# Leaving rows of zero weight out of the gathers of a routed expert layer, made head by head, with five added rows in eight on TensorE

## The chip, the cores and the metric

The kernel runs on one core of one Trainium2 chip. The metric is the time of the core on the device in microseconds (us), from the first to the last instruction. Three runs of the kernel before were made, and their median is what the changed kernel is compared with.

## The reference, cut to what matters

A model of several blocks on 256 tokens of width 2048 in float32: an attention block, a Fourier mixer, a convolution and state-space mixer, a cross attention, and at the end a layer of routed experts. Only the last is touched. In it each of 8 heads picks 16 of 128 x 128 experts for each token, so a token has 128 experts; each expert is one row of 2048 numbers in a table `u_tab` (here called scored rows) and one in a table `v_tab` (added rows):

```python
g = jax.nn.softmax(top_s, axis=-1)                 # of the 16 best scores of a head
u = jnp.take(u_tab, it, axis=0)                    # scored rows, one per token and slot
act = jax.nn.gelu(jnp.einsum("td,tkd->tk", xt, u))
v = jnp.take(v_tab, it, axis=0)                    # added rows
return jnp.einsum("tk,tkd->td", gt * act, v)       # weight = gt * act
```

The inputs are random, and several are multiplied by a factor: the gain of the layer's norm by 8, the scored table by 3.246, the query weights by 2.935, the keys by 2.911. A weight `gt * act` is exactly zero in float32 where gelu of a negative product is, or where the softmax term vanishes. The result goes through a last norm.

## The kernel before

Everything ahead of the expert stage is untouched and ends some 2100 us into the run. The stage (class `Experts`, functions `g_experts`, `v_experts`, `a_experts`, `pe_experts`) treats the 256 tokens as two tiles (t = 0, 1) of 128 tokens, one token per SBUF partition. For each tile there are 128 slots k (`E_SLOTS`), 16 (`TOPK`) for each of 8 heads. A gather is one indirect DMA that GpSimd (POOL) issues (L3784): for one (t, k) it brings one row of 8 KB for each of 128 tokens, from `in_peer_u` (table 0, scored) or `in_peer_v` (table 1, added). There are 512. They go into twelve buffers of 8 KB per partition (four in `arena`, eight in `ring`), used in a fixed rotation; a gather waits until what its buffer held was used.

`ORDER`, written by `gather_order`, is the one order in which all engines go through the gathers: first `LAG` = 36 scored ones, then one added and one scored in turn, and at the end added ones alone (36).

- VectorE (DVE) sums a scored row against the token's input with one instruction (`v_scored`, L3698), which gives one product per token in `X.act`.
- When the 32 scored rows of two heads are done, ScalarE (ACT) applies gelu to their 32 products (L3741), and DVE, just before the first added row of those two heads, multiplies them by the softmax terms (L3681). These are the weights.
- An added row is taken by DVE, as weight x row + sum in place (L3686), or by TensorE (PE): ACT builds a diagonal matrix of the weights (L3750, four buffers `diag`), and PE multiplies it by the row into four PSUM banks (L3554, four calls, each of which is two instructions in the trace). Of eight slots, `PE_ROWS` = 1, 4 and 6 go to PE.
- Between them DVE makes the choice of experts for the next two heads in small steps (`v_choose`, L3566 to L3646), whose integer row numbers `X.idx` the gathers read.
- When the last added row of a tile is done, `v_finish` adds PE's sums to DVE's, takes the norm and scales (L3709 to L3715), and the tile is stored.

In the kernel before, an added gather waits only for the row numbers and for its buffer, not for the weights.

Of the kernel before, what the change touches and what calls it, by code (L numbers as in the profile page):

```python
# [39 lines left out]
HH = 2  # L40
# [3344 lines left out]
class Experts:  # L3385
    def __init__(self, c):
        W = c.I["peer_w_q_2"][0]
        n = HH * 2 * E_HALF
        self.q_lins = [Lin(f"peer_q{g}", W, g * n, (g + 1) * n) for g in range(GROUPS)]
        self.H = c.at(0, NT, D)  # L3390
        self.hn = c.at(4 * K1, NT, D)
        self.x = c.at(8 * K1, KD * SEQ)
        self.f_row = c.at(10 * K1, D)
        self.g_row = c.at(12 * K1, D)
        self.rs = c.st[:, 62:64]
        self.qT = c.at(12 * K1, E_HEADS, SEQ)
        self.keys = c.at(14 * K1, E_HEADS, E_KEYS)
        self.sc = c.at(15 * K1, HH * 2, E_KEYS)
        self.cand = c.at(15 * K1 + 512, HH, TOPK, TOPK)
        self.eq = c.at(16 * K1, HH, TOPK, TOPK)  # L3400
        small = c.at(21 * K1, 16, 256)
        self.v1 = small[:, 0, :]
        self.i1 = small[:, 1, :].bitcast(U32)
        self.i1f = small[:, 2, :]
        self.top = small[:, 3, 0:E_SLOTS]
        self.pos = small[:, 4, 0:E_SLOTS].bitcast(U32)
        self.pi = small[:, 5, 0:E_SLOTS].bitcast(U32)
        self.pj = small[:, 6, 0:E_SLOTS].bitcast(U32)
        self.pif, self.pjf = small[:, 7, 0:E_SLOTS], small[:, 8, 0:E_SLOTS]
        self.e1, self.e2 = small[:, 9, 0:E_SLOTS], small[:, 10, 0:E_SLOTS]  # L3410
        self.idxf = small[:, 11, 0:E_SLOTS]
        self.hsum = small[:, 12, 0:E_HEADS]
        self.g = c.at(25 * K1, NT, E_SLOTS)
        self.act = c.at(25 * K1 + 256, NT, E_SLOTS)
        self.idx = c.at(25 * K1 + 512, NT, E_SLOTS).bitcast(U32)
        self.bufs = [c.ring[:, i // 2, (i % 2) * D:(i % 2 + 1) * D] for i in range(2 * RING)] + [
            c.at(17 * K1, D), c.at(19 * K1, D), c.at(26 * K1, D), c.at(28 * K1, D)]
        self.buf_of = {}
        self.tables = (c.I["peer_u_2"][0], c.I["peer_v_2"][0])
        self.sums, self.added, self.diag_holder = {}, None, {}  # L3420

    def diag_of(self, t, k):

        return sum(1 for j in range(k) if on_pe(j)) % 4

    def cols(self, k):
        return self.x[:, k * SEQ:(k + 1) * SEQ]
# [3 lines left out]
        return [key for q in (ch // 4, ch // 4 + 1) for key in turn_free(("ffn_x", q), 4, NT)]  # L3431


LAG = HH * TOPK + 4
PE_ROWS = (1, 4, 6)


def gather_order():
# [10 lines left out]
ORDER = gather_order()  # L3449


def on_pe(k):

    return k % 8 in PE_ROWS


LAST_PE_ROW = max(k for k in range(E_SLOTS) if on_pe(k))


def choice_at(t, k):  # L3460
# [69 lines left out]
def pe_experts(c):  # L3530
    nc, pe, X = c.nc, c.pe, c.experts
    last_rows = pe_ffn_rows(c)(KD // 4 - 1)
    for h in range(HH):
        yield from pe_queries(c, X, h, 1, None if h else last_rows)
        yield from pe_choose(c, X, 0, h, 1)
    for h in range(HH, E_HEADS, HH):
        yield from pe_queries(c, X, h, HH)
        if h == HH:
            yield from pe_choose(c, X, 0, h)
    for n, (t, table, k) in enumerate(ORDER):  # L3540
        if table == 0:
            choice = choice_at(t, k)
            if choice is not None and choice[2] == 0 and choice[:2] != (0, 1):
                yield from pe_choose(c, X, choice[0], choice[1] * HH)
            continue
        if k == PE_ROWS[0]:
            X.sums[t] = []
            for b in range(4):
                bank = yield from pe_bank(c, c.lin, ("rows", t, b))
                X.sums[t].append(bank)  # L3550
        if on_pe(k):
            yield from pe.wait_ge(("diag", t, k), ("got", t, 1, k))
            for b in range(4):
                mm = nc.tensor.matmul(X.sums[t][b][:, :], c.diag[:, X.diag_of(t, k), :],  # L3554
                                      X.buf_of[t, 1, k][:, b * 512:(b + 1) * 512],
                                      start=(k == PE_ROWS[0]), stop=(k == LAST_PE_ROW), skip_group_check=True)
            names = [("full", ("rows", t))] if k == LAST_PE_ROW else []
            mm.then_inc(c.pe_full.after(("row_used", t, 1, k), *names), 1)


# [95 lines left out]
def v_experts(c):  # L3656
    nc, v, X, step = c.nc, c.v, c.experts, c.v_step
    vt = nc.vector.tensor_tensor
    yield from v_ffn_rows(c, KD // 4 - 1)
    yield from v_ffn_gained(c, KD // 4 - 1)  # L3660
    yield from v_rms(c, "ffn_x", ("y_mem", "squares"))
    nc.vector.tensor_copy(X.rs, c.st[:, 0:NT]).then_inc(step.after(("ffn_x", "scale")), 1)
    for h in range(HH):
        if h == 0:
            yield from v_copy_out(c, ("query", h), X.qT[:, h, :], lambda: c.bank[("query", h)][:, 0:SEQ])
        v.side = [v_choose(c, X, 0, h, 1)]
        yield from v.aside(0)
    for n, (t, table, k) in enumerate(ORDER):
        if table == 0:
            yield from v_scored(c, X, t, k)  # L3670
            choice = choice_at(t, k)
            if choice is not None:
                if choice[2] == 0:
                    v.side = [v_choose(c, X, choice[0], choice[1] * HH)]
                yield from v.aside(1)
            continue
        group = k // (HH * TOPK)
        if k % (HH * TOPK) == 0:
            ks = slice(k, k + HH * TOPK)
            yield from v.wait_ge(("gelu", t, group))  # L3680
            nc.vector.tensor_tensor(X.act[:, t, ks], X.act[:, t, ks], X.g[:, t, ks], ALU.mult).then_inc(  # L3681
                step.after(("weights", t, group)), 1)
            yield from v.wait_ge(step)
        if not on_pe(k):
            yield from v.wait_ge(("got", t, 1, k), X.added)
            nc.vector.scalar_tensor_tensor(out=X.H[:, t, :], in0=X.buf_of[t, 1, k], scalar=X.act[:, t, k:k + 1],  # L3686
                                           in1=X.H[:, t, :], op0=ALU.mult, op1=ALU.add).then_inc(
                c.v_out.after(("row_used", t, 1, k)), 1)
            X.added = ("row_used", t, 1, k)
        if k == E_SLOTS - 1:  # L3690
            yield from v_finish(c, X, t)


def v_scored(c, X, t, k):
    yield from c.v.wait_ge(("got", t, 0, k))
    buf = X.buf_of[t, 0, k]
    names = [("scored", t, k // (HH * TOPK))] if k % (HH * TOPK) == HH * TOPK - 1 else []
    c.nc.vector.tensor_tensor_reduce(out=buf, in0=buf, in1=X.hn[:, t, :], scale=1.0, scalar=0.0, op0=ALU.mult,  # L3698
                                     op1=ALU.add, accum_out=X.act[:, t, k:k + 1]).then_inc(
        c.v_out.after(("row_used", t, 0, k), *names), 1)  # L3700
# [18 lines left out]
def a_experts(c):  # L3719
# [10 lines left out]
    for h in range(HH, E_HEADS, HH):  # L3730
        yield from a_copy_out(c, ("query", h), X.qT[:, h:h + HH, :], lambda: pairs(c.bank[("query", h)][:, :]))
    for n, (t, table, k) in enumerate(ORDER):
        group = k // (HH * TOPK)
        if table == 0:
            choice = choice_at(t, k)
            if choice is not None and choice[2] == 9:
                yield from a_choose(c, X, choice[0], choice[1] * HH)
            if k % (HH * TOPK) == HH * TOPK - 1:
                ks = slice(k + 1 - HH * TOPK, k + 1)
                yield from a.wait_ge(("scored", t, group))  # L3740
                nc.scalar.activation(X.act[:, t, ks], X.act[:, t, ks], ACT.Gelu_apprx_tanh, scale=X.rs[:, t:t + 1]).then_inc(  # L3741
                    c.a_step.after(("gelu", t, group)), 1)
                if (t, group) == (NT - 1, GROUPS - 1):
                    yield from a_root_ahead(c)
            continue
        if on_pe(k):
            q = X.diag_of(t, k)
            yield from a.wait_ge(("weights", t, group), X.diag_holder.get(q))
            X.diag_holder[q] = ("row_used", t, 1, k)
            nc.scalar.activation(c.diag[:, q, :], c.ident[:, :], ACT.Copy, scale=X.act[:, t, k:k + 1]).then_inc(  # L3750
                c.a_step.after(("diag", t, k)), 1)
# [12 lines left out]
def g_experts(c):  # L3764
# [13 lines left out]
    for n, (t, table, k) in enumerate(ORDER):  # L3778
        m = n - FIRST_ROUNDS * len(early)
        q = early[n % len(early)] if m < 0 else order[m % len(order)]  # L3780
        yield from g.wait_ge(("idx", t, k // TOPK), holder.get(q))
        holder[q] = ("row_used", t, table, k)
        X.buf_of[t, table, k] = X.bufs[q]
        c.nc.gpsimd.indirect_dma_start(  # L3784
            X.bufs[q], None, X.tables[table],
            bass.IndirectOffsetOnAxis(ap=X.idx[:, t, k:k + 1], axis=0)).then_inc(got[q].after(("got", t, table, k)), 16)


def program(nc, I, out):
# [151 lines left out]
```

## Time and profile before

| | |
|---|---|
| runs | 3407.87, 3407.84, 3405.35 us, median 3407.84 |
| span of the profiled execution | 3407.9 us; the time of its run lies within 0.1 us of it |
| DMA in the expert stage | 421 to 422 GB/s |
| DVE busy in the whole span | 2503.4 us |
| POOL busy in the whole span | 1497.5 us |
| PE busy in the whole span | 2574.2 us |

The profile is of one execution. Times are in us from the start of the span, durations of single instructions in ns where marked. In the slices a digit is the busy share in tenths (9 is 90% or more), each slice being a fortieth of the span, 85.2 us. PEclk is the clock granted to TensorE, DMA the mean busy share of the core's 16 DMA engines. The duration of a DMA instruction on POOL is the time in which POOL makes its descriptors, not the transfer; the time to landing is the transfer with its queue.

### The profile page before, as it was taken

How to read it: one execution, taken by the hardware profiler on the slowest of the kernel's cores; microseconds unless marked ns; L12 is line 12 of the kernel's file. 1: busy time of each engine (PE TensorE's matmuls, PEld its weight loads, DVE VectorE, ACT ScalarE, POOL GpSimd, SP SyncE). 2: the span in 40 equal slices, each digit the busy share in tenths (PEclk: the TensorE clock that was granted, in tenths of full speed). 3: DMA queues.
4: the chain of work that ended last, by engine and by line, in shares of the span. 5: the costliest groups of instructions: out<-in, count | busy, mean ns of one | idle time of the engine just before them, and what ended most of it. 6: DMA issues, size and time to landing. Idle time of an engine off the chain costs nothing.

```text
span 3407.9 us, 32819 instructions
## 1 busy us (share of the span) xinstructions
PE 2574.2 (76%) x11844; PEld 1856.5 (54%) x11844; DVE 2503.4 (73%) x3758; ACT 1004.3 (29%) x1999; POOL 1497.5 (44%) x1973
## 2 busy tenths in 40 slices
PE   6999999999999999999999999144444444444445
PEld 4678886557888887887677888111111111111112
DVE  5568887756677765568756557997878888888775
ACT  5364263233555444444155442000000001000000
POOL 6678888700000000002200002887777767777663
PEclk9999999999999999999999999576766766676778
DMA  9967766525477755554635556999999999999998
GB/s 377 387 233 288 251 216 230 222 105 181 151 246 248 233 189 179 173 200 164 188 132 174 172 174 241 412 422 422 421 421 422 422 421 414 420 421 422 421 422 333
DMA packets 297858, 986.05 MB, mean 289 GB/s; under 512 B 15456, under 2 KB 139744, under 8 KB 213216
## 3 DMA queue, kind: packets, MB, share of 16 engines
q0 software_dynamic: 77024, 555.78, 39.4%
q1 hardware_dynamic: 216448, 417.56, 35.7%
q10 hardware_dynamic: 4224, 10.62, 0.8%
q8 instruction: 93, 1.52, 0.2%
q14 instruction: 69, 0.57, 0.1%
HBM read 965.94 MB, written 17.96 MB: 289 GB/s over the span
## 4 chain that ended last, share of the span: by engine, by line
PE 52%; DMA 17%; DVE 14%; POOL 10%; issue 4%; ACT 3%; SPq 0%; ACTq 0%; DVEq 0%
PE lin L568 12%; DMA ring<-in_peer_v,arena 7%; POOL ring L3784 7%; PE lin L493 6%; PE lin L495 6%; PE lin L494 6%; PE lin L570 6%; DMA ring<-in_peer_u,arena 4%; PE lin L394 3%; POOL arena L3784 3%; PE lin L3554 3%; DMA arena<-in_peer_u,arena 3%; DMA arena<-in_peer_v,arena 3%; DVE scratch L915 2%; DVE weight_parts L451 2%
## 5 line engine op out<-in xcount | busy, mean ns | idle before, releaser
L451 DVE TENSOR_TENSOR weight_parts<-ring,weight_parts 128x512 fp32r<-128x512 f32 (+2 forms) x994 | 671.5, 689 | 468.5 <-ACT weight_parts L439 463.8
L439 ACT CAST weight_parts<-ring 128x512 fp32r<-128x512 f32 (+2 forms) x994 | 593.4, 607 | 699.1 <-PE lin L495 357.9
L3554 PE MATMUL lin<-ring,scratch 128*128 128x512 f32 x512 | 362.0, 873 | 493.9 <-DMA ring<-in_peer_v,arena 372.5
L568 PE MATMUL lin<-parts,weight_parts 128*128 128x512 f32 x1792 | 643.3, 402 | 12.6 <-DVE weight_parts L451 9.8
L3554 PEld LDWEIGHTS lin<-ring,scratch 128*128 128x128 f32 x512 | 140.1, 287 | 712.6 <-issue 656.5
L570 PE MATMUL lin<-parts,weight_parts 128*128 128x256 f32 x1792 | 503.4, 281 | 0.0
L3698 DVE CUSTOM_DVE_ANT_0 ring<-ring,arena 128x2048 f32<-128x2048 f32 x168 | 383.3, 2289 | 92.3 <-DMA ring<-in_peer_u,arena 86.4
L493 PE MATMUL lin<-weight_parts,parts 128*128 128x512 f32 (+2 forms) x1092 | 419.1, 384 | 24.4 <-DVE weight_parts L451 16.8
L3784 POOL DMA_INDIRECT ring<-in_peer_u,arena x168 | 301.5, 1795 | 306.3 <-DVE arena L3571 231.3
L494 PE MATMUL lin<-weight_parts,parts 128*128 128x512 f32 (+2 forms) x1092 | 410.3, 376 | 0.0
L495 PE MATMUL lin<-weight_parts,parts 128*128 128x512 f32 (+2 forms) x1092 | 410.1, 376 | 0.0
L568 PEld LDWEIGHTS lin<-parts,weight_parts 128*128 128x128 f32 x1792 | 338.8, 189 | 111.2 <-DVE weight_parts L451 16.6
L3784 POOL DMA_INDIRECT ring<-in_peer_v,arena x172 | 303.7, 1766 | 160.4 <-PE lin L3554 112.4
L3554 PE MATMUL lin<-arena,scratch 128*128 128x512 f32 x256 | 178.9, 864 | 217.0 <-DMA arena<-in_peer_v,arena 186.8
L570 PEld LDWEIGHTS lin<-parts,weight_parts 128*128 128x128 f32 x1792 | 340.6, 190 | 0.4
L3686 DVE SCALAR_TENSOR_TENSOR arena<-ring,arena 128x2048 f32<-128x2048 f32 x108 | 253.6, 2348 | 33.9 <-DMA ring<-in_peer_v,arena 32.5
L493 PEld LDWEIGHTS lin<-weight_parts,parts 128*128 128x128 f32 x1092 | 207.9, 190 | 76.4 <-DVE weight_parts L451 23.1
L3554 PEld LDWEIGHTS lin<-arena,scratch 128*128 128x128 f32 x256 | 69.6, 286 | 325.3 <-issue 288.7
L1094 POOL DMA_DIRECT2D arena<-mem_turned x3 | 1.6, 541 | 539.2 <-PE aux L2323 529.0
L3698 DVE CUSTOM_DVE_ANT_0 arena<-arena 128x2048 f32<-128x2048 f32 x88 | 200.9, 2288 | 50.8 <-DMA arena<-in_peer_u,arena 47.9
L495 PEld LDWEIGHTS lin<-weight_parts,parts 128*128 128x128 f32 x1092 | 207.9, 190 | 36.7
L494 PEld LDWEIGHTS lin<-weight_parts,parts 128*128 128x128 f32 x1092 | 207.8, 190 | 35.5 <-issue 1.2
(329 smaller groups left out, 3846.1 us busy)
## 6 DMA issues: line engine op xcount, KB each, us to landing
ring<-in_ada_row_loads SPq DMA_DIRECT2D x64, 1024.0 KB, 8.3
ring<-in_w_in_fourier SPq DMA_DIRECT2D x64, 1024.0 KB, 8.4
ring<-in_ada_front_loads SPq DMA_DIRECT2D x32, 1024.0 KB, 8.6
ring<-in_w_in_attn SPq DMA_DIRECT2D x32, 1024.0 KB, 7.0
ring<-in_w_out_fourier SPq DMA_DIRECT2D x16, 2048.0 KB, 8.0
ring<-in_w_in SPq DMA_DIRECT2D x24, 1024.0 KB, 7.4
ring<-in_mem_k_loads SPq DMA_DIRECT2D x16, 1024.0 KB, 10.9
ring<-in_w_out_attn SPq DMA_DIRECT2D x8, 2048.0 KB, 7.9
```

The lines of the kernel that those rows point to most:

```text
L394: mm = c.nc.tensor.matmul(banks[j // 2][:, (j % 2) * SEQ:(j % 2 + 1) * SEQ], wt[:, k % L.kc, j * P:(j + 1) * P], rhs(k), start=(k == 0 and ...
L439: c.nc.scalar.copy(c.w_parts[:, q, 0, 0:L.per * w], weights_of(c, L, load, w, k)).then_inc(c.a_high.after(("high", L.name, i)), 1)
L451: c.nc.vector.tensor_tensor(c.w_parts[:, q, 1, 0:L.per * w], weights_of(c, L, load, w, k), c.w_parts[:, q, 0, 0:L.per * w].bitcast(F32), A ...
L493: c.nc.tensor.matmul(banks[t][:, 0:w], lhs(0, k, t), hi, start=(k % part == 0), stop=False)
L494: c.nc.tensor.matmul(banks[t][:, 0:w], lhs(0, k, t), lo, start=False, stop=False)
L495: mm = c.nc.tensor.matmul(banks[t][:, 0:w], lhs(1, k, t), hi, start=False, stop=(k % part == part - 1))
L568: c.nc.tensor.matmul(pairs(banks[j][:, :]), c.w_parts[:, q, 0, b], x, start=(k == 0), stop=False, skip_group_check=True)
L570: mm = c.nc.tensor.matmul(banks[j][:, hi_at * SEQ:(hi_at + 1) * SEQ], c.w_parts[:, q, 1, b], x[:, hi_at, :], start=False, stop=(k == L.K - ...
L3554: mm = nc.tensor.matmul(X.sums[t][b][:, :], c.diag[:, X.diag_of(t, k), :], X.buf_of[t, 1, k][:, b * 512:(b + 1) * 512], start=(k == PE_ROW ...
L3686: nc.vector.scalar_tensor_tensor(out=X.H[:, t, :], in0=X.buf_of[t, 1, k], scalar=X.act[:, t, k:k + 1], in1=X.H[:, t, :], op0=ALU.mult, op1 ...
L3698: c.nc.vector.tensor_tensor_reduce(out=buf, in0=buf, in1=X.hn[:, t, :], scale=1.0, scalar=0.0, op0=ALU.mult, op1=ALU.add, accum_out=X.act[ ...
L3784: c.nc.gpsimd.indirect_dma_start(X.bufs[q], None, X.tables[table], bass.IndirectOffsetOnAxis(ap=X.idx[:, t, k:k + 1], axis=0)).then_inc(go ...
```

## The change

1. Weights are made for each head (16 slots) and not for two heads, and sooner: `weights_at` places them four places behind the head's last scored row in `ORDER` (`WEIGHTS_BEHIND` = 4), in a new function `v_weights`. ACT's gelu is applied for each head as well.
2. `v_weights` then compares the weights with zero, gives zero ones a row number out of the table (`NO_ROW`, 4 x 128 x 128) and writes the row numbers of the head anew, as integers.
3. Added gathers wait for these row numbers (`rows_needed`) and carry a bounds check: a row number above 16383 brings no row, and the buffer keeps what it held there. Its weight is zero.
4. Five of eight added rows are PE's (slots 1, 2, 4, 6, 7) in place of three; in the last 32 added rows, behind which no scored ones stand, it is three as before.
5. 32 scored gathers stand ahead of the first added one, not 36, and so 32 added ones are alone at the end.

```diff
-LAG = HH * TOPK + 4
-PE_ROWS = (1, 4, 6)
+LAG = 2 * TOPK
+PE_ROWS = (1, 2, 4, 6, 7)
+PE_ROWS_ALONE = (1, 4, 6)
+WEIGHTS_BEHIND = 4
+NO_ROW = 4 * E_KEYS * E_KEYS
...
+def on_pe(t, k):
+
+    alone = (t, k) >= (NT - 1, E_SLOTS - LAG)
+    return k % 8 in (PE_ROWS_ALONE if alone else PE_ROWS)
...
+def weights_at(n):
+
+    last = [(t, 0, k) for t in range(NT) for k in range(TOPK - 1, E_SLOTS, TOPK)]
+    done = ORDER[n - WEIGHTS_BEHIND] if n >= WEIGHTS_BEHIND else None
+    return (done[0], done[2] // TOPK) if done in last else None
...
     for n, (t, table, k) in enumerate(ORDER):
+        due = weights_at(n)
+        if due is not None:
+            yield from v_weights(c, X, *due)
...
-        group = k // (HH * TOPK)
-        if k % (HH * TOPK) == 0:
-            ks = slice(k, k + HH * TOPK)
-            yield from v.wait_ge(("gelu", t, group))
-            nc.vector.tensor_tensor(X.act[:, t, ks], X.act[:, t, ks], X.g[:, t, ks], ALU.mult).then_inc(
-                step.after(("weights", t, group)), 1)
-            yield from v.wait_ge(step)
-        if not on_pe(k):
+        if not on_pe(t, k):
...
+def v_weights(c, X, t, h):
+
+    nc, v, step = c.nc, c.v, c.v_step
+    ks = slice(h * TOPK, (h + 1) * TOPK)
+    yield from v.wait_ge(("gelu", t, h))
+    nc.vector.tensor_tensor(X.act[:, t, ks], X.act[:, t, ks], X.g[:, t, ks], ALU.mult).then_inc(
+        step.after(("weights", t, h)), 1)
+    yield from v.wait_ge(step)
+    nc.vector.tensor_scalar(X.skip, X.act[:, t, ks], 0.0, float(NO_ROW), ALU.is_equal, ALU.mult).then_inc(step.after(), 1)
+    yield from v.wait_ge(step)
+    nc.vector.tensor_tensor(X.idxf[:, ks], X.idxf[:, ks], X.skip, ALU.max).then_inc(step.after(), 1)
+    yield from v.wait_ge(step)
+    nc.vector.tensor_copy(X.idx[:, t, ks], X.idxf[:, ks]).then_inc(step.after(("rows_needed", t, h)), 1)
...
-        c.nc.gpsimd.indirect_dma_start(
-            X.bufs[q], None, X.tables[table],
-            bass.IndirectOffsetOnAxis(ap=X.idx[:, t, k:k + 1], axis=0)).then_inc(got[q].after(("got", t, table, k)), 16)
+        if table == 0:
+            yield from g.wait_ge(("idx", t, k // TOPK), holder.get(q))
+            c.nc.gpsimd.indirect_dma_start(X.bufs[q], None, X.tables[0], rows).then_inc(
+                got[q].after(("got", t, 0, k)), 16)
+        else:
+            yield from g.wait_ge(("rows_needed", t, k // TOPK), holder.get(q))
+            c.nc.gpsimd.indirect_dma_start(X.bufs[q], None, X.tables[1], rows, bounds_check=E_KEYS * E_KEYS - 1,
+                                           oob_is_err=False).then_inc(got[q].after(("got", t, 1, k)), 16)
```

## Rows read from the trace of the kernel before

**Rows 1.** Page, 40 slices of the span: POOL, DMA share and rate.

```profile
POOL 6678888700000000002200002887777767777663
DMA  9967766525477755554635556999999999999998
GB/s 377 387 233 288 251 216 230 222 105 181 151 246 248 233 189 179 173 200 164 188 132 174 172 174 241 412 422 422 421 421 422 422 421 414 420 421 422 421 422 333
```

**Rows 2.** Busy time of each engine in the four stretches of the stage.

```profile
core 0: us, PE busy (x) PEld busy (x) DVE busy (x) ACT busy (x) POOL busy (x), PEclk, DMA share, GB/s
2102.00:2185.00 83.00, 38.28 (x187) 32.94 (x185) 80.89 (x157) 3.67 (x6) 62.46 (x36) 0.75 0.98 398
2185.00:3279.00 1094.00, 471.71 (x683) 183.97 (x684) 921.24 (x1024) 50.64 (x117) 808.89 (x440) 0.68 1.01 421
3279.00:3370.00 91.00, 53.47 (x93) 21.38 (x92) 58.69 (x33) 6.59 (x16) 52.98 (x37) 0.79 1.01 421
3370.00:3408.00 38.00, 18.95 (x35) 7.03 (x33) 22.42 (x20) 3.49 (x10) 0.58 (x1) 0.80 0.54 222
```

**Rows 3.** Page, DMA queue of POOL: packets, MB, share of 16 engines.

```profile
q0 software_dynamic: 77024, 555.78, 39.4%
```

**Rows 4.** Line 3784 (gathers): duration ns min/median/max, first and last start; landing.

```profile
L3784 POOL DMA_INDIRECT ring<-in_peer_v,arena x172: 932/1894/5215, 2185.4 to 3369.6; - x172
L3784 POOL DMA_INDIRECT ring<-in_peer_u,arena x168: 933/1906/5215, 2102.1 to 3279.2; - x168
DMA to landing us min/median/max: 6.6/23.6/26.7
```

**Rows 5.** Windows of 2400 to 3200: all engines, then lines 3698 and 3686.

```profile
2400.00:3200.00 800.00, 353.07 (x508) 137.79 (x509) 670.77 (x753) 38.30 (x89) 582.22 (x321) 0.68 1.01 421
...
2400.00:3200.00 800.00, 364.21 (x319) 0.68 1.01 421
...
2400.00:3200.00 800.00, 232.92 (x100) 0.68 1.01 421
```

**Rows 6.** Timeline, DVE and POOL, 2130 to 2136: start us, us.

```profile
2130.68 2.28 DVE L3698 CUSTOM_DVE_ANT_0 ring<-ring,arena 128x2048 f32<-128x2048 f32 x1
2130.82 2.95 POOL L3784 DMA_INDIRECT ring<-in_peer_u,arena  x1 [0.30 <-issue]
2132.89 2.28 DVE L3698 CUSTOM_DVE_ANT_0 arena<-arena 128x2048 f32<-128x2048 f32 x1
2134.08 1.91 POOL L3784 DMA_INDIRECT ring<-in_peer_u,arena  x1 [0.30 <-issue]
2135.10 0.86 DVE L3581 MAX8 arena<-arena 128x8 f32<-128x128 f32 x4
```

**Rows 7.** Timeline, DVE and POOL, 2503 to 2506.

```profile
2503.71 0.94 POOL L3784 DMA_INDIRECT arena<-in_peer_v,arena  x1 [0.30 <-issue]
2504.95 0.94 POOL L3784 DMA_INDIRECT arena<-in_peer_u,arena  x1 [0.30 <-issue]
2505.27 2.29 DVE L3698 CUSTOM_DVE_ANT_0 ring<-ring,arena 128x2048 f32<-128x2048 f32 x1 [2.68 <-DMA ring<-in_peer_u,arena]
```

**Rows 8.** Timeline of PE, an added row's instructions after a pause and later.

```profile
2512.86 3.38 PE L3554 MATMUL lin<-ring,scratch 128*128 128x512 f32 x4 [2.44 <-DMA ring<-in_peer_v,arena]
...
3372.49 3.67 PE L3554 MATMUL lin<-arena,scratch 128*128 128x512 f32 x8 [1.30 <-DMA arena<-in_peer_v,arena]
```

**Rows 9.** Lines 3681 (weights) and 3750 (diagonals): duration ns min/median/max.

```profile
L3681 DVE TENSOR_TENSOR arena<-arena x8: 183/186/191, 2210.0 to 3316.6; 128x32 f32<-128x32 f32 x8
...
L3750 ACT ACTIVATE scratch<-ident,arena x96: 384/386/403, 2210.2 to 3371.2; 128x128 f32<-128x128 f32 x96
```

**Rows 10.** Chain that ended last, its end: start us, us.

```profile
3369.64 24.98 DMA ring<-in_peer_v,arena
...
3394.65 2.36 DVE arena L3686
...
3397.10 0.70 DVE arena L3709
```

More of the change, by code:

```diff
@@ L3412, in __init__ @@
         self.hsum = small[:, 12, 0:E_HEADS]
+        self.skip = small[:, 13, 0:TOPK]
         self.g = c.at(25 * K1, NT, E_SLOTS)
@@ L3422, in diag_of @@
     def diag_of(self, t, k):
-        return sum(1 for j in range(k) if on_pe(j)) % 4
+        return sum(1 for j in range(k) if on_pe(t, j)) % 4
     def cols(self, k):
@@ L3449 @@
 ORDER = gather_order()
-def on_pe(k):
-    return k % 8 in PE_ROWS
-LAST_PE_ROW = max(k for k in range(E_SLOTS) if on_pe(k))
+def on_pe(t, k):
+    alone = (t, k) >= (NT - 1, E_SLOTS - LAG)
+    return k % 8 in (PE_ROWS_ALONE if alone else PE_ROWS)
+LAST_PE_ROW = [max(k for k in range(E_SLOTS) if on_pe(t, k)) for t in range(NT)]
+def weights_at(n):
+    last = [(t, 0, k) for t in range(NT) for k in range(TOPK - 1, E_SLOTS, TOPK)]
+    done = ORDER[n - WEIGHTS_BEHIND] if n >= WEIGHTS_BEHIND else None
+    return (done[0], done[2] // TOPK) if done in last else None
 def choice_at(t, k):
@@ L3550, in pe_experts @@
                 X.sums[t].append(bank)
-        if on_pe(k):
+        if on_pe(t, k):
             yield from pe.wait_ge(("diag", t, k), ("got", t, 1, k))
@@ L3555, in pe_experts @@
                                       X.buf_of[t, 1, k][:, b * 512:(b + 1) * 512],
-                                      start=(k == PE_ROWS[0]), stop=(k == LAST_PE_ROW), skip_group_check=True)
-            names = [("full", ("rows", t))] if k == LAST_PE_ROW else []
+                                      start=(k == PE_ROWS[0]), stop=(k == LAST_PE_ROW[t]), skip_group_check=True)
+            names = [("full", ("rows", t))] if k == LAST_PE_ROW[t] else []
             mm.then_inc(c.pe_full.after(("row_used", t, 1, k), *names), 1)
@@ L3696, in v_scored @@
     buf = X.buf_of[t, 0, k]
-    names = [("scored", t, k // (HH * TOPK))] if k % (HH * TOPK) == HH * TOPK - 1 else []
+    names = [("scored", t, k // TOPK)] if k % TOPK == TOPK - 1 else []
     c.nc.vector.tensor_tensor_reduce(out=buf, in0=buf, in1=X.hn[:, t, :], scale=1.0, scalar=0.0, op0=ALU.mult,
@@ L3732, in a_experts @@
     for n, (t, table, k) in enumerate(ORDER):
-        group = k // (HH * TOPK)
+        h = k // TOPK
         if table == 0:
@@ L3737, in a_experts @@
                 yield from a_choose(c, X, choice[0], choice[1] * HH)
-            if k % (HH * TOPK) == HH * TOPK - 1:
-                ks = slice(k + 1 - HH * TOPK, k + 1)
-                yield from a.wait_ge(("scored", t, group))
+            if k % TOPK == TOPK - 1:
+                ks = slice(k + 1 - TOPK, k + 1)
+                yield from a.wait_ge(("scored", t, h))
                 nc.scalar.activation(X.act[:, t, ks], X.act[:, t, ks], ACT.Gelu_apprx_tanh, scale=X.rs[:, t:t + 1]).then_inc(
-                    c.a_step.after(("gelu", t, group)), 1)
-                if (t, group) == (NT - 1, GROUPS - 1):
+                    c.a_step.after(("gelu", t, h)), 1)
+                if (t, h) == (NT - 1, E_HEADS - 1):
                     yield from a_root_ahead(c)
             continue
-        if on_pe(k):
+        if on_pe(t, k):
             q = X.diag_of(t, k)
-            yield from a.wait_ge(("weights", t, group), X.diag_holder.get(q))
+            yield from a.wait_ge(("weights", t, h), X.diag_holder.get(q))
             X.diag_holder[q] = ("row_used", t, 1, k)
@@ L3780, in g_experts @@
         q = early[n % len(early)] if m < 0 else order[m % len(order)]
-        yield from g.wait_ge(("idx", t, k // TOPK), holder.get(q))
+        rows = bass.IndirectOffsetOnAxis(ap=X.idx[:, t, k:k + 1], axis=0)
+        X.buf_of[t, table, k] = X.bufs[q]
+        if table == 0:
[6 more added lines that the diff above has]
+                                           oob_is_err=False).then_inc(got[q].after(("got", t, 1, k)), 16)
         holder[q] = ("row_used", t, table, k)
-        X.buf_of[t, table, k] = X.bufs[q]
-        c.nc.gpsimd.indirect_dma_start(
-            X.bufs[q], None, X.tables[table],
-            bass.IndirectOffsetOnAxis(ap=X.idx[:, t, k:k + 1], axis=0)).then_inc(got[q].after(("got", t, table, k)), 16)
 def program(nc, I, out):
```

## The prediction

> **What bounds the kernel now.** I read the 40 slices first, to find where the changed code runs. In the slices from the 26th on, the DMA engines are nine tenths or more busy and move about 422 GB/s; that is the expert stage, the only one whose code differs [rows 1]. Then the windows cut at the stage's own joints: 2102 to 2185 (scored rows alone), 2185 to 3279 (an added row and a scored row in turn), 3279 to 3370 (the last added rows) and the end. In the second the DMA engines are full (share 1.01), DVE is busy for 921 of 1094 us, POOL for 809 and PE for 472 [rows 2]. The reader is to see that the transfers set the pace and that three other engines stand at 43 to 84%. 220 added and 220 scored gathers go in 1094 us, so a pair takes 4.97 us, and one gather of 128 rows of 8 KB (1.0486 MB) takes 2.49 us at 421 GB/s. The queue of POOL's transfers confirms it: 555.8 MB, of which the 512 gathers are 536.9 [rows 3]. A gather lands a median 23.6 us after its issue, some nine gathers of 2.49 us deep [rows 4]. So POOL runs ahead of the transfers, and a saving of bytes is a saving of time until another engine is as slow.
>
> **The bytes that go.** An added row is left out when its weight is exactly zero. The trace can't show how many are, so I took the reference's arithmetic with its inputs. The normalised input has a gain of about 8 and the scored table a factor of 3.246, so the products have a spread of 8 x 3.246 = 26, and gelu is zero in float32 below about -5.2: two fifths of a spread of 26 lies there (the normal share below -0.2 is 42%). Evaluated on the inputs, 44.0% of the 32,768 weights are zero, 2 points of it from softmax terms that vanish. That is 14,400 rows. In single gathers it is 30 to 58%. It assumes that the engine's gelu and exp reach exact zero at about those places. An added gather then takes 0.56 x 2.49 = 1.39 us, and a pair 2.49 + 1.39 = 3.88 us of the DMA engines. Over 256 added gathers 256 x 0.44 x 2.49 = 280 us of transfer go. If nothing else bound, the time would be 3408 - 280 = 3128 us.
>
> **DVE.** In 2400 to 3200 it is busy 670.8 us for 161 pairs, 4.17 us each; 364.2 are the scored rows' sums (2.29 each) and 232.9 the added rows (2.35 each) [rows 5]. Three added rows in eight stay on DVE in place of five: 0.25 x 2.35 = 0.59 us less in a pair. The new weights take four small instructions for a head of 16 rows where one of 0.19 us stood for 32 [rows 9]; at 0.19 each with their waits some 0.8 us a head, 0.05 a pair. So 4.17 - 0.59 + 0.05 = 3.63 us: below 3.88, no bound by itself.
>
> **PE.** An added row is eight instructions. Four that follow a pause take 3.38 us, 0.85 each, and all eight of a row on a busier engine 3.67 us, 0.46 each [rows 8]; the granted clock is 0.68 on average in the stage [rows 2], between the two levels of 1.2 and 2.4 GHz. Five rows in eight are 0.625 x 3.67 = 2.3 us a pair at the high level and 0.625 x 6.8 = 4.2 us if all were at the low one. Now it is 472 us over the 82.5 rows of 220 pairs that PE has, 5.7 us a row; the rest of the work lies closer together afterwards, so I take 5 us a row, 3.1 a pair, no bound. ACT's diagonals at 0.39 us each are nothing [rows 9].
>
> **POOL, the next bound.** Here is where I expect the saving to be cut. A gather's instruction takes 0.93 us when nothing holds it, but 1.9 as a median [rows 4], 1.81 as the mean in 2400 to 3200 (582.2 / 321) [rows 5]. The timeline shows why: one that starts during a long DVE instruction ends some 0.8 to 0.9 us after that instruction's end (start 2130.82, DVE's next starts at 2132.89, the gather ends at 2133.77; the following one ends at 2135.99, 0.89 after 2135.10) [rows 6]. One that starts in a gap takes 0.94 [rows 7]. Between two there are 0.30 us. So POOL issues about one gather per long DVE instruction, and one per 0.94 + 0.30 = 1.24 us of other time. A pair has 1 + 0.375 = 1.375 long ones, 2.29 + 0.88 = 3.17 us, and needs two gathers. At best the other 0.625 cost 0.625 x 1.24 = 0.78 us: 3.95 us a pair. At worst starts fall at random: now long ones cover 597.1/800 = 0.746 of the time and add 0.88 us to a gather, 1.18 per unit of cover; with T us for a pair, T = 2 x 1.24 + 2 x 1.18 x 3.17/T, which gives 4.24. Both are above the transfers' 3.88. Now the same sum gives 2 x (1.81 + 0.30) = 4.22 of 4.97 us, which is why it doesn't show.
>
> The Trainium skill ("SBUF — State Buffer", section "Who interferes with whom") says that GpSimd and a VectorE instruction with two SBUF inputs contend for one pair of ports, and that the later one is fully blocked; for POOL the trace agrees. It would hold VectorE as well when the gather came first. By that, the 0.625 gathers a pair that start in gaps would add up to 0.94 us each to DVE, 3.63 + 0.59 = 4.2 us a pair, the same sum as below. But a DVE instruction that starts within such a gather, at 2505.27, still takes 2.29 us [rows 7], so I give this no more than 1 in 100.
>
> **Transfers are uneven too.** Each of 16 engines carries eight of 128 rows. If always the same eight, zero weights fall on them by chance: over six pairs (twelve buffers) the fullest engine has, by the mask, 81 rows where the mean is 75, 8% more. With all of it lost, a pair is 3.88 x 1.08 = 4.19 us; over the whole stage the fullest has 2% more, 3.96. Two limits of about 4 us that share buffers add a little to each other. I take T = 4.2 for the pair.
>
> **Waits that the order adds.** An added gather must now wait for its head's weights. With 32 scored ahead, head h's added rows begin at place 32 + 32h of the order; its last scored row is at place 15, 31, then 32h - 1, and its weights are made four places later. Twelve buffers let POOL be at most twelve places ahead of what was used, so before place 32 + 32h is issued place 20 + 32h has been used, behind the weights for every head (place 19 for head 0). Cost nothing. What is queued behind a late weight on POOL would be all gathers of both tables, up to 25 us, but no place comes near. The gelu instruction runs 16 times for 8, and its table comes twice in two heads as now, since exp comes once.
>
> **The sum**, against the profiled execution: its span of 3407.9 us, which the runs' 3407.84 and 3407.87 match. Gathers begin at 2102.1; the first added one was issued at 2185.4 [rows 4] and is due four gathers earlier, 2185.4 - 4 x 2.49 = 2175.4. 224 pairs x 4.2 = 941. Then 32 added rows alone, 20 on DVE: at best 0.625 x 2.35 + 0.375 x 1.24 = 1.93 us each, at worst (the same random sum) 2.08; 2.0 x 32 = 64. Behind the last issue now stand 38.3 us: 25.0 to land in a full queue, 2.4 for the row and 10.8 for the finish [rows 10]; with the queue short I take 9 for the landing (its least is 6.6 [rows 4]): 22. Sum 2175 + 941 + 64 + 22 = 3202; I say 3200.
>
> **Rivals.** (a) The transfers alone pace it, POOL falling into step at 3.95 or below: T 3.88 to 4.05, 3128 to 3165 us. For it: POOL hits gaps well when DVE must wait. 0.2. (b) POOL or PE is dearer than I take: the bounds test adds 0.2 to 0.4 us to an added gather's instruction, 3200 + 256 x 0.3 = 3277, or PE stays at its low level, where 4.2 us a pair is a third limit equal to T, and the three together cost 0.2 more: 3200 + 224 x 0.2 = 3245. Nothing in the trace prices the test; from the nearest rows it is between nothing and the whole step from 0.93 to 1.9. 0.15. (c) Leaving rows out doesn't shorten the transfer, or gelu isn't exactly zero: the pair stays at 4.97 and the time within a few us of 3408. Against it: the queue carries 536.9 MB in 65,536 rows of 8 KB, so its packets follow the rows [rows 3]. 0.05. (d) Slower: POOL is the bound, so each us that the test adds counts once per added gather. It decides from 208 / 256 = 0.81 us; at 1.5 us the time is 3200 + 384 = 3584. The instruction is 0.93 us for 128 rows now, so it would have to nearly double. 0.07. (e) My forecast, 3165 to 3230: 0.53.
>
> **How the numbers follow.** The likeliest is 3200. The range 3130 to 3280 takes in (a), (b) and (e), 0.88 of which I think some falls outside at its edges. Faster (over 0.2%, what a measurement of this kernel can tell) 0.88, same 0.05, slower 0.07.
>
> **What would show it.** The queue of POOL's transfers falls by 14,400 packets and 118 MB. DVE's added rows go from 160 to 84 + 20 = 104, PE's from 96 to 152. In the middle stage the DMA share falls below 1, to about 0.93, at 390 GB/s; landing falls from 23.6 to 8 to 15 us; POOL has hardly a wait for PE or DVE left, and its idle time before a gather is the bare 0.30. The unblocked gather of the added table still takes 0.93 us. I am wrong if DMA stays at 1 with the queue deep (a or c), if added gathers take over 1.2 us unblocked (b, d), or if POOL waits for the new weights' conversion on DVE.

## The result, and the profile after

The changed kernel takes 3234.97 us (median of 4 runs, 3231.22 to 3248.85), the kernel before 3406.88 us beside it (4 runs): a ratio of 0.9504, 95% interval 0.9482 to 0.9527, faster by 5%. The forecast was 3200 us with a range of 3130 to 3280. The profiled execution took 3231.22 us, its span is 3229.6.

The page's slices, POOL, the DMA engines' share and rate, beside [rows 1]:

```profile
POOL 6677787740000000000220000078888888888886
DMA  9977676525558674545563554599999999999997
GB/s 378 387 258 284 227 245 228 234 95 205 176 171 269 225 238 172 182 169 202 180 173 128 183 183 165 186 413 384 399 372 385 407 361 409 368 375 406 391 385 269
```

The busy time of each engine in the paired part, and in 800 us of it, beside [rows 2, 5]:

```profile
2170.00:3100.00 930.00, 597.52 (x1096) 239.37 (x1096) 789.55 (x1011) 73.29 (x178) 794.17 (x427) 0.82 0.97 387
...
2250.00:3050.00 800.00, 524.46 (x968) 209.70 (x966) 677.56 (x864) 66.21 (x158) 682.64 (x368) 0.84 0.97 388
```

POOL was busy for 73% of the middle part and is now busy for 85%. With 0.31 us between two gathers, 368 of them account for 682.6 + 114 = 797 of 800 us. The lines of the gathers (L3812 added, L3808 scored: duration ns min/median/max, first and last start), what ended the idle time ahead of the added ones, and their landing, beside [rows 4]:

```profile
L3812 POOLq MOVE  x256: 29/29/39, 2166.3 to 3195.2; - x128
L3812 POOL DMA_INDIRECT ring<-in_peer_v,arena x172: 986/1970/5280, 2176.2 to 3208.7; - x172
L3812 POOL DMA_INDIRECT arena<-in_peer_v,arena x84: 986/1972/5277, 2167.3 to 3193.4; - x84
...
  issue: 75.0, 246
  PE lin L3566: 3.1, 8
...
DMA to landing us min/median/max: 6.5/9.7/14.8
```

```profile
L3808 POOL DMA_INDIRECT ring<-in_peer_u,arena x168: 933/1838/5151, 2092.3 to 3133.1; - x168
L3808 POOL DMA_INDIRECT arena<-in_peer_u,arena x88: 933/1843/5152, 2094.9 to 3142.9; - x88
```

Two things are to be read. POOL goes from gather to gather with the bare 0.3 us of issue, and from the first added gather on its longer waits come to 6 us in all: it is hardly ever behind anybody. And a gather lands 9.7 us after its issue, where it was 23.6: the queue that POOL used to be ahead of is gone. The share of 0.97 alone would still have pointed at the transfers; an experiment decides on that below.

The page's counts of packets, and POOL's queue, beside [rows 3]:

```profile
DMA packets 297864, 877.43 MB, mean 272 GB/s; under 512 B 28731, under 2 KB 153019, under 8 KB 226491
...
q0 software_dynamic: 77024, 447.08, 35.1%
```

108.7 MB fewer move, 13,275 rows of 8 KB. The number of packets is what it was.

**Where the 178.3 us between the two spans are.** The first gather starts 9.8 us sooner (2092.3 for 2102.1), in code that is the same; eleven profiles of this study have it between 2092.3 and 2107.6, without a pattern, so this part of the difference is no effect of the change. From the first to the last issue it was 1267.5 us and is 1116.4: 151.1 less. From the last issue to the end it was 38.3 and is 20.9 (3229.6 - 3208.7): 17.4 less. Below I give stage times, from the first gather to the end of the span: 1305.8 before, 1137.3 after.

### The profile page after: what moved, and what is told of

Read it like the earlier page. It is cut to its first block, busy times and chain, and to the rows that moved or that the text cites. A ratio compares the mean times of both kernels' runs of the same rounds, so it can differ in the third digit from the quotient of the medians.

```text
span 3229.6 us, 34045 instructions
## 1 busy us (share of the span) xinstructions
PE 2700.1 (84%) x12292; PEld 1910.1 (59%) x12292; DVE 2377.8 (74%) x3758; ACT 1029.3 (32%) x2065; POOL 1514.2 (47%) x1973
## 2 busy tenths in 40 slices
DMA packets 297864, 877.43 MB, mean 272 GB/s; under 512 B 28731, under 2 KB 153019, under 8 KB 226491
## 4 chain that ended last, share of the span: by engine, by line
PE 53%; POOL 15%; DVE 13%; issue 10%; DMA 6%; ACT 3%; SPq 0%; ACTq 0%; POOLq 0%; DVEq 0%
PE lin L568 12%; PE lin L493 6%; PE lin L570 6%; PE lin L495 6%; PE lin L494 6%; POOL ring L3812 5%; POOL ring L3808 4%; PE lin L394 4%; POOL arena L3812 3%; POOL arena L3808 2%; DMA ring<-in_peer_v,arena 2%; PE lin L3566 2%; DVE scratch L915 2%; DMA ring<-in_peer_u,arena 2%; DVE weight_parts L451 2%
## 5 line engine op out<-in xcount | busy, mean ns | idle before, releaser
L3566 PE MATMUL lin<-ring,scratch 128*128 128x512 f32 x808 | 464.0, 732 | 251.3 <-DMA ring<-in_peer_v,arena 204.9
L3566 PEld LDWEIGHTS lin<-ring,scratch 128*128 128x128 f32 x808 | 184.2, 237 | 526.8 <-issue 468.4
L3808 POOL DMA_INDIRECT ring<-in_peer_u,arena x168 | 295.4, 1759 | 292.0 <-DVE arena L3583 230.8
L3812 POOL DMA_INDIRECT ring<-in_peer_v,arena x172 | 325.5, 1892 | 52.4 <-issue 51.2
L3566 PE MATMUL lin<-arena,scratch 128*128 128x512 f32 x408 | 215.5, 680 | 155.6 <-DMA arena<-in_peer_v,arena 87.9
L3566 PEld LDWEIGHTS lin<-arena,scratch 128*128 128x128 f32 x408 | 86.0, 219 | 283.2 <-issue 258.7
L3773 ACT ACTIVATE scratch<-ident,arena 128x128 f32<-128x128 f32 x152 | 55.1, 394 | 494.1 <-PE lin L3566 494.1
```

The lines of the kernel that those rows point to most:

```text
L3808: c.nc.gpsimd.indirect_dma_start(X.bufs[q], None, X.tables[0], rows).then_inc(got[q].after(("got", t, 0, k)), 16)
L3812: c.nc.gpsimd.indirect_dma_start(X.bufs[q], None, X.tables[1], rows, bounds_check=E_KEYS * E_KEYS - 1, oob_is_err=False).then_inc(got[q].a ...
```

## The experiments

All are edits of the changed kernel, whose time is 3235 us. The interval in brackets is that of the ratio to the kernel before. "A pair" is the time from the first added gather's instruction to the last scored one's, over 223.5: 4.37 us after the change ((3142.9 - 2166.3) / 223.5, 2166.3 being where the first added gather's own MOVE starts), 4.98 before, (3279.2 - 2185.4) / 219.5. The expectations' formula, T = 2.54 + 2.5 x L / T with L the us of long DVE instructions in a pair, is the prediction's random sum with two unheld gathers of 0.93 and 0.99 us, twice 0.31 between, and the factor fitted to the changed kernel's 4.36 at L = 3.17.

**1. No row left out.**

```diff
-NO_ROW = 4 * E_KEYS * E_KEYS
+NO_ROW = 0
```

> The changed kernel with the row number that marks a zero weight set to 0, so that no row is ever left out; the four small instructions per head, the bounds test, the order and the five rows in eight on TensorE stay. Nothing of the computation is left out. If the gain comes from the bytes alone (my theory), the pair of gathers is back at 4.97 us of transfer, the queue at nine or ten gathers, and the time at 3395 to 3410 us. The rival that the move of rows to TensorE or the earlier weights bring part of the gain by themselves gives under 3380 us. The bounds test with no row out of bounds: if a gather of the added table still takes 0.99 us unheld, the 0.05 us more is the test and not the leaving out.

Measured 3406.89 us, ratio 0.999 (0.9979 to 1.0002): without the leaving out there is no gain; the move of rows to TensorE and the early weights bring nothing by themselves. (Once the bytes are gone the move does count: experiment 3.) The slices are full at 422 GB/s again:

```profile
GB/s 367 391 237 289 249 219 232 223 105 179 153 243 251 232 188 180 174 196 167 188 135 169 177 171 240 413 422 422 421 422 422 422 422 422 422 422 422 422 422 332
```

The least duration of an added gather's instruction is 989 ns and of a scored one's 937 here, with no row out of bounds. So the test costs 0.05 us, and leaving rows out neither adds to POOL's time nor takes from it.

**2. All added rows left out.**

```diff
-... X.act[:, t, ks], 0.0, float(NO_ROW), ALU.is_equal, ALU.mult)
+... X.act[:, t, ks], 0.0, float(NO_ROW), ALU.mult, ALU.add)
```

> The changed kernel with every added row marked as left out: all 256 added gathers are issued but bring nothing, so the sum of the added rows is left out of the computation. Theory P (POOL's issuing sets the pace, 2 x (1.855 + 0.31) = 4.33 us a pair in the profile): POOL has the same instructions and DVE the same long ones, so the pair stays at 4.2 to 4.4 us and the time at 3205 to 3240 us although 161 MB fewer move. Theory D (the transfers, 387 GB/s at a share of 0.97, or their unevenness over 16 engines, set it): the transfer of a pair falls from about 3.97 to 2.6 us, the next limit is DVE at 3.8, and the time is 3235 - 224 x 0.5 = 3120 us or less.

Measured 3237.03 us (0.947 to 0.9502), the same as the changed kernel with 160 MB less. Its windows:

```profile
2250.00:3050.00 800.00, 511.37 (x964) 207.62 (x965) 681.43 (x889) 65.93 (x157) 686.63 (x373) 0.84 0.72 246
```

The DMA share falls from 0.97 to 0.72 and the rate to 246 GB/s, and nothing else moves: POOL has 687 us for 373 gathers, DVE 681. This refutes the transfers as the limit, their unevenness over the engines with them. A pair is 4.35 us.

**3. Three rows in eight on TensorE.**

```diff
-PE_ROWS = (1, 2, 4, 6, 7)
+PE_ROWS = (1, 4, 6)
```

> The changed kernel with three of eight added rows on TensorE, as before the change; the leaving out stays. Theory P: 1.625 long DVE instructions a pair (3.76 us) in place of 1.375 (3.17 us) hold POOL more often; with T = 2.54 + 2.5 x 3.76 / T the pair is 4.59 us for 4.36, 224 x 0.23 = 51 us more, 3286 us. Theory D: DVE is at about 4.3 of 4.36 us and the bytes are the same, so 3235 to 3245 us.

Measured 3271.18 us (0.9571 to 0.9603), 36 us more where 51 were expected and 0 to 10 by the rival. So of the 172 us gained, 36 need both parts of the change. The pair is 4.50 us by its trace, not 4.59. POOL has no time left here (689.0 + 357 x 0.31 = 800 us); its mean gather of 1.93 us is 0.97 above the mean least of 0.96, at a cover (the share of time under long DVE instructions) of 3.76 / 4.50 = 0.836. That is 1.16 per unit of cover, where the formula's 2.5 has 1.25 for each of two gathers: the holding grew less than the formula has it. DVE, at 756 of 800 us, is close behind:

```profile
2250.00:3050.00 800.00, 375.33 (x578) 148.06 (x579) 756.18 (x921) 46.20 (x105) 689.01 (x357) 0.71 0.95 374
```

**4. The bounds test on the scored gathers too.**

```diff
-            c.nc.gpsimd.indirect_dma_start(X.bufs[q], None, X.tables[0], rows)
+            c.nc.gpsimd.indirect_dma_start(X.bufs[q], None, X.tables[0], rows,
+                                           bounds_check=E_KEYS * E_KEYS - 1, oob_is_err=False)
```

> The changed kernel with the bounds test on the scored gathers too; every row number of theirs is in bounds, so nothing else changes. Theory P: each of 256 scored gathers takes about 0.05 us more on POOL (0.99 in place of 0.93 unheld, ends 0.87 in place of 0.81 us behind the DVE instruction that held it), which counts in full: 13 to 15 us more, 3248 to 3250 us. Theory D: nothing, 3235 us.

Measured 3241.76 us (0.9485 to 0.9528, which holds the changed kernel's own 0.9504), stage 1139.1 us for 1137.3, pair 4.37 us as in the changed kernel. A miss for my theory as I had put it, and what the rival expected, though experiment 2 rules that rival out: 256 instructions that are 0.05 us longer when unheld don't add 13 us. A few us the times can't exclude; the pair of the trace shows none. The reading that fits is in the next section.

**5. Six, seven and eight rows in eight on TensorE** (three in eight in the last 32 rows, as in the changed kernel).

```diff
-PE_ROWS = (1, 2, 4, 6, 7)
+PE_ROWS = (1, 2, 3, 4, 6, 7)                 # six
+PE_ROWS = (1, 2, 3, 4, 5, 6, 7)              # seven
+PE_ROWS = (0, 1, 2, 3, 4, 5, 6, 7)           # eight
```

> The changed kernel with six of eight added rows on TensorE. By POOL's sum 1.25 long DVE instructions a pair (2.88 us): T = 2.54 + 2.5 x 2.88 / T = 4.24 us, 27 us less than with five, 3205 to 3212 us. Rival as for seven rows: no gain.

> The changed kernel with seven of eight added rows on TensorE. If POOL's issuing is paced by the long DVE instructions, 1.125 of them a pair (2.58 us) in place of 1.375 (3.17 us) give T = 2.54 + 2.5 x 2.58 / T = 4.11 us for 4.36, so 56 us less, 3175 to 3185 us; PE has 0.875 x 3.67 = 3.2 us a pair at its high clock. Rival: the transfers (1.0486 MB x 1.595 at 422 GB/s, 3.96 us, and up to 8% more by unevenness, 4.28 us) or PE below its high clock (0.875 x 5 = 4.4 us) take over, and the time stays within 20 us of 3235.

> The changed kernel with all added rows on TensorE except in the last 32, where it is three in eight as before. One long DVE instruction a pair, 2.29 us: T = 2.54 + 2.5 x 2.29 / T = 3.98 us by POOL, but the transfers are at 3.96 us and PE at 3.67 us at its high clock, so three limits meet: 4.05 to 4.15 us a pair, 3165 to 3190 us. Rival: TensorE falls behind with a row in every pair and holds the buffers (POOL then shows long waits for PE), and the time is above that of seven rows.

Measured 3213.88 us for six (0.9407 to 0.9438), 3184.75 for seven (0.9327 to 0.9358), 3182.49 for eight (0.9317 to 0.9348). The pairs are 4.24, 4.09 and 4.12 us where the sum gave 4.24, 4.11 and, with three limits meeting, 4.05 to 4.15. The sixth row in eight pays 21 us and the seventh 29, until other limits are reached. The windows of seven and of eight, one after the other:

```profile
2250.00:3050.00 800.00, 655.94 (x1408) 273.78 (x1407) 607.46 (x846) 88.19 (x214) 665.86 (x393) 0.92 1.01 412
```

```profile
2250.00:3050.00 800.00, 711.91 (x1600) 297.77 (x1601) 551.02 (x828) 98.04 (x237) 636.08 (x390) 0.97 1.01 410
```

With seven the DMA share is 1.01 and POOL is still nearly full (665.9 + 393 x 0.31 = 788 us). With eight POOL has room (636.1 + 390 x 0.31 = 757 us), the transfers have not, and PE is at 712 us: the eighth row brings nothing. The waits for PE that the rival named do appear, and the time is still not above that of seven rows. These are POOL's waits for it in the paired part of eight (us, times, longest):

```profile
POOL ring L3812 <- PE lin L3566: 20.0, 16, 3.6
POOL arena L3812 <- PE lin L3566: 12.2, 9, 3.7
```

PE was not the bound of the changed kernel: it was busy for 524 of 800 us there, and more rows on it made the kernel faster. The clock granted to it rose from 0.84 to 0.92 and 0.97 with the moved rows.

**6. A short instruction behind an added row's.** On DVE, behind each added row's instruction in the paired part:

```diff
             X.added = ("row_used", t, 1, k)
+            if n // 2 < 240:
+                nc.vector.memset(X.spare[:, n // 2:n // 2 + 1], 0.0)
```

> The changed kernel with one short DVE instruction (a fill of one number per partition) behind each of the 84 added rows that DVE takes in the paired part. In the profile 13 gathers of 5.2 us stayed held over the end of an added row's instruction, each time where the next long one followed at once. If a short instruction between the two lets POOL in, these gathers go (none over 4 us), which frees 13 x 2.3 = 30 us of POOL for 84 x 0.06 = 5 us of DVE: 10 to 25 us less, 3210 to 3225 us. If the held ones have another cause they stay, and the time is 3235 to 3240 us.

Measured 3219.83 us (0.9436 to 0.9479, just below the changed kernel's 0.9482 to 0.9527), 15 us less than the changed kernel, pair 4.27 us for 4.37. DVE has more work here and the time falls, so DVE's own time is not the bound either. The timelines of the two kernels at the same place of the program (start us, us):

```profile
2511.51 2.33 DVE L3694 SCALAR_TENSOR_TENSOR arena<-ring,arena 128x2048 f32<-128x2048 f32 x1
2511.65 5.27 POOL L3812 DMA_INDIRECT arena<-in_peer_v,arena  x1 [0.30 <-DVE arena L3598]
2513.76 2.28 DVE L3721 CUSTOM_DVE_ANT_0 ring<-ring,arena 128x2048 f32<-128x2048 f32 x1
```

```profile
2508.84 2.33 DVE L3695 SCALAR_TENSOR_TENSOR arena<-ring,arena 128x2048 f32<-128x2048 f32 x1
2508.97 3.07 POOL L3815 DMA_INDIRECT arena<-in_peer_v,arena  x1 [0.30 <-DVE arena L3599]
2511.10 2.28 DVE L3724 CUSTOM_DVE_ANT_0 ring<-ring,arena 128x2048 f32<-128x2048 f32 x1
2511.12 0.06 DVE L3700 MEMSET arena<- 128x1 f32 x1
```

In the first, the gather starts 0.14 us into an added row's instruction, isn't let in at its end, and ends 0.88 us behind the end of the next (2516.92, the next having ended at 2516.04). In the second, with the fill issued between the two (the trace has its start 0.02 us behind that of the second long one), it ends 0.87 us behind the first. In the changed kernel's trace 77 gathers start during an added row's instruction with a scored one right behind it, and 13 of them go this way; in this run it is 79 and none, and the longest of all takes 3.10 us. At the end of a scored one's instruction no gather was ever passed over, in any of the traces: a second instruction of 0.08 us on DVE, which reads out the sum, always follows it.

**7. Short scored sums.** On top of experiment 2, the scored rows are summed over 1024 of their 2048 numbers. The result lacks the added rows and half of each sum.

```diff
-... tensor_tensor_reduce(out=buf, in0=buf, in1=X.hn[:, t, :],
+... tensor_tensor_reduce(out=buf[:, 0:D // 2], in0=buf[:, 0:D // 2], in1=X.hn[:, t, 0:D // 2],
```

> As the run in which every added row is left out (3237 us, the added rows are missing from the result), and the scored rows are summed over their first 1024 of 2048 numbers only, so half of each scored sum is left out as well. The gathers and their number are the same; the DVE instruction of a scored row is 1.2 us for 2.29. If the length of the DVE instructions sets POOL's pace, T = 2.54 + 2.5 x (1.2 + 0.88) / T = 3.88 us for 4.35 a pair, 105 us less, 3120 to 3145 us. If POOL is held by something of its own or of the transfers (a queue of descriptors, the landing), the pair stays at 4.35 us and the time at 3225 to 3240 us.

Measured 3034.71 us (0.889 to 0.8919), 202 us below experiment 2 where 105 were expected, with a pair of 3.52 us for 4.35. Nothing of POOL's own was changed, and its gathers became shorter:

```profile
L3812 POOL DMA_INDIRECT ring<-in_peer_v,arena x172: 989/1003/4207, 2172.7 to 3016.6; - x172
```

The median of the added gathers' instruction in `ring` fell from 2.00 us (experiment 2) to 1.00, the least stayed. So the length of DVE's instructions does set POOL's pace; the sum that I carried through the experiments is only good while that length stays (next section).

## Why the prediction was right, point by point

**The mechanism held.** The transfers bounded the kernel before (experiment 1 gives its time back), and once the bytes go, POOL's issuing is the bound, held by DVE's long instructions (experiments 2, 3, 5 and 7 together; experiment 2 excludes rival (a), and rival (c) falls with the result itself, which moves 108.7 MB less). The landing (9.7 us, forecast 8 to 15) and POOL's waits are as forecast.

**The sum, term by term.** The first added gather was due at 2175.4; it came at 2166.3, of which 9.8 us are the untouched part, which leaves 0.7. The 224 pairs were put at 4.2 us, 941 us; they take 4.37, 979 us: this is the term that was mis-sized, by 38 us. The last 32 rows were put at 64 us and take 65.8 (3142.9 to 3208.7). The end was put at 22 and takes 20.9. So the profiled execution misses the sum of 3202 by -9, +38, +2 and -1 us, which gives 3232; its span is 3229.6, since from the first added to the last scored gather there are 223.5 pairs and not 224. The -9 is chance; the median of the runs, 3235, is above the profiled one.

**What was wrong in the pair.** I had the bounds 3.95 and 4.24 and the step "I take T = 4.2", and the measured 4.37 lies above both. The random sum had 0.88 us of holding for a gather at a cover of 0.746, 1.18 per unit. After the change the cover is 3.17 / 4.37 = 0.725 and the mean instruction 682.6 / 368 = 1.855 us, 0.895 above the mean least of 0.96: 1.23 per unit. With 1.23 and the 0.05 us of the test the sum gives 4.34 us; POOL's waits of 6 us are 0.03 a pair and make it 4.37. Nearly half of the rise from 1.18 to 1.23 is the window that I had read: over the whole paired part of the kernel before, the mean gather is 808.9 / 440 = 1.84 us, 0.905 above its least, at a cover of 3.76 / 4.97 = 0.756 [rows 2], which is 1.20, and the sum would have given 4.31 with the test. The rest isn't settled. The factor is no constant: the same working gives 1.16 for three rows and for seven, 1.21 for six, and 1.12 in experiment 6. The gathers held twice, which experiment 6 has no more, are part of the holding (15 us by the times, 0.07 us a pair), but they are in the 1.18 as well. The best case of 3.95, with a gather in every gap, is far off: in a gap a gather starts only when the one before has ended. Starts at random describe it much better.

**The bounds test** was priced "between nothing and the whole step". It is 0.05 us when nothing holds the gather. It pays in the sum only as far as a gather isn't held: a held one ends at a time that DVE sets, and if the next is also held, what the instruction itself takes is hidden in that wait. Experiment 4 showed less than the 13 us for 256 more tests, and no more time in the pair; this explanation is argued from the timeline, not shown by a run of its own. Rivals (b) and (d) are out as far as they rest on the test. That PE is a third limit, the other half of (b), is out by experiment 5.

**Whether a gather holds DVE.** The prediction gave this 1 in 100. It is out: in the changed kernel 78 scored sums start inside a gather that nothing holds, and they take 2.29 us in the mean, as the other 178 do.

**The lengths.** Experiment 7 missed by a factor of two because a held gather waits for the rest of an instruction, which grows with its length, and is held more often, which does too. With the square of the length the numbers join: 2.5 us per us of long instructions holds for 2.3 us ones; for those of 1.2 us it is about 2.5 x 1.2 / 2.3 = 1.3; T = 2.54 + (1.3 x 1.2 + 2.5 x 0.88) / T gives 3.59, measured 3.52. This was worked out afterwards.

**The zeros.** I took 44.0% of the weights as exactly zero from the reference's arithmetic; 13,275 of 32,768 rows are left out, 40.5%. I had written that this assumed where the engine's gelu and exp reach exact zero; whether one of them, and which, explains the 3.5 points was not tried. Since the transfers don't bound any longer it costs nothing here. "The queue falls by 14,400 packets" was wrong in kind too: the packets stay, and those left out turn small (under 512 B: 28,731, where the page had 15,456 before). They are nearly free: between 2250 and 3050 us a packet under 512 B takes 9 ns in the mean, and all of them together are 0.01 of the DMA share in the changed kernel and 0.02 in experiment 2.

**The DMA share.** Forecast were 0.93 and 390 GB/s; measured are 0.97 and 387. The rate is near by two misses that offset: more bytes a pair, 2.49 x 1.595 = 3.97 us of transfer and not 3.88, over a longer pair. The share is higher than the rate asks for, and in experiment 2 still more so (0.72, where 246 GB/s would be 0.59 by the 421 GB/s at 1.01 of before). By the traces the packets of 8 KB take longer, 314 ns in the mean before, 326 after the change and 376 in experiment 2, with a median that doesn't grow (313, 309 and 309). Why some of them take longer was not tried. So 0.97 at 388 GB/s overstated how near to full the transfers were; seven rows in eight moved 412.

**DVE, PE and waits.** Added rows on DVE are 104 and on PE 152 by their counts. The four small instructions take 0.17 to 0.18 us each in the median, where 0.19 was taken. DVE is busy for 677.6 us over 184 pairs, 3.68 us each, forecast 3.63; PE for 524.5, 2.85 us a pair or 4.6 a row, where 3.1 and 5 were taken. PE's least instruction is 592 ns both times; in `ring` the median fell from 1048 to 592 and the mean from 873 to 732 as the granted clock rose (0.68 to 0.82 in the paired part). No gather waited for the new row numbers in a way that the trace shows: POOL's waits for DVE are 0.6 us ahead of the added gathers. Costing the order at nothing was right.

Luck has a part in the number: 3235 lies 5 us above what I had called my own forecast, (e), 3165 to 3230. The time lies in the range because this reached up to the dearer pair of rival (b), 3277; the time of (b) came about without its cause.

**A better version.** Seven rows in eight on TensorE takes 3184.75 us and eight 3182.49, both faster than the changed kernel by 50 us or more (1.6%) and than the kernel before by 6.6%; between them there is no difference that the runs tell. With seven, no gather is held twice any more (the longest takes 3.1 us), so I didn't add the short instruction of experiment 6 to it.

## What to carry to other kernels

When a transfer-bound stage is relieved of bytes, do the sum of the engine that issues the transfers before any other: its instructions may be short by themselves and long because another engine's hold them, and this shows only as a median far above the minimum. Then the lever is the other engine: here it was fewer or shorter long sums on VectorE, even at the price of more on TensorE. A DMA share of 0.97 does not say that the transfers are the limit; leave them out once and see whether the time moves.

## What the runs showed of the hardware that I had not expected

- A gather's row whose number is out of bounds still makes a packet, of less than 512 B and 9 ns in the mean, and POOL's instruction is no shorter for it (least 0.986 us with two fifths left out, 0.989 with none).
- The bounds test costs 0.05 us for a gather of 128 rows (0.937 against 0.989).
- At the end of an added row's instruction on DVE, with a scored one right behind, POOL is sometimes not let in (13 of 512 gathers, up to 5.28 us); a fill of 0.06 us between the two ended this (none over 3.10 us).
- The holding goes one way: a gather of 0.93 us grows up to 5 us beside DVE's long sums, and a long sum that starts inside an unheld gather keeps its 2.29 us.
- Untouched stages put the start of the gathers anywhere from 2092.3 to 2107.6 us in eleven executions, 15 us that a single profile must not be read for.
